# One of the six low parts of each expert chunk is made by GpSimd instead of VectorE

## The reference, cut to what matters

```
def swiglu(h, wg, wu, wd):
    a = jnp.einsum('bsd,df->bsf', h, wg)
    b = jnp.einsum('bsd,df->bsf', h, wu)
    return jnp.einsum('bsf,fd->bsd', jax.nn.silu(a) * b, wd)

def moe_swiglu(h, router_w, wg, wu, wd):
    ...
    for e in range(N_EXPERTS):
        out = out + combine[..., e:e + 1].astype(h.dtype) * swiglu(h, wg[e], wu[e], wd[e])
```

## Time and profile before

| | us |
|---|---|
| median of 3 runs | 1541.75 (1541.41 to 1542.61) |
| the profiled execution: its own time | 1544.39 |
| its span, first to last instruction | 1542.6 |
| expert stage, roughly | from 540 to 1528 |
| one plain step of six tiles | 17.0 |
| one scatter step | 18.9 |

### The profile page before, as it was taken

The page is one execution under the profiler, slowest core; times in us unless marked ns, Lnnn a source line. Parts: engine busy times, 40 slices in busy tenths (PEclk is TensorE's granted clock), DMA queues, the critical chain, the costliest instruction groups (busy, mean ns, idle before and its releaser), DMA issues.

```text
span 1542.6 us, 19268 instructions
## 1 busy us (share of the span) xinstructions
PE 1503.1 (97%) x7347; PEld 1243.0 (81%) x7347; DVE 1190.7 (77%) x881; ACT 975.6 (63%) x742; POOL 11.0 (1%) x26
## 2 busy tenths in 40 slices
PE   7999999999999999999999999999999999999996
PEld 5987788888888678888878888887888888888885
DVE  4777454444787588898888889888889888888885
ACT  4565433344556477777767776776777777777774
POOL 2000000000000000000000000000000000000000
PEclk9999999999999999999999999999999999999998
DMA  9624555554552279999999999999999998999991
GB/s 312 217 96 139 177 191 189 189 190 137 178 177 96 96 271 387 372 361 360 376 324 336 373 375 351 369 335 327 373 366 350 372 376 316 359 365 377 355 375 61
DMA packets 190583, 437.70 MB, mean 284 GB/s; under 512 B 9328, under 2 KB 13472, under 8 KB 190384
## 3 DMA queue, kind: packets, MB, share of 16 engines
q1 hardware_dynamic: 189024, 432.90, 78.0%
q0 software_dynamic: 1056, 2.19, 0.7%
q10 hardware_dynamic: 432, 1.57, 0.3%
HBM read 435.59 MB, written 1.05 MB: 283 GB/s over the span
## 4 chain that ended last, share of the span: by engine, by line
PE 91%; DVE 4%; issue 2%; ACT 2%; DMA 1%; SPq 0%; DVEq 0%; ACTq 0%
PE ps L1219 28%; PE ps L1221 28%; PE ps L1220 28%; PE ps L1523 2%; DVE w_lo L1068 1%; DVE w_lo L760 1%; PE ps L1480 1%; PE ps L1498 1%; DMA raw<-in_w_in_dram 1%; PE ps L1499 1%; ACT w_hi L584 0%; PE ps L1282 0%; PE ps L1281 0%; PE ps L1280 0%; ACT w_hi L440 0%
## 5 line engine op out<-in xcount | busy, mean ns | idle before, releaser
L1068 DVE TENSOR_TENSOR w_lo<-raw,w_hi 128x2048 fp32r<-128x2048 f32 x333 | 754.1, 2288 | 111.9 <-ACT w_hi L584 110.9
L584 ACT ACTIVATE w_hi<-raw 128x2048 fp32r<-128x2048 f32 x332 | 630.4, 1920 | 171.7 <-PE ps L1221 171.7
L1219 PE MATMUL ps<-w_hi,aT_hi 128*128 128x512 f32 (+1 forms) x1296 | 512.8, 396 | 13.9 <-DVE w_lo L760 6.1
L1221 PE MATMUL ps<-w_hi,aT_lo 128*128 128x512 f32 (+1 forms) x1296 | 504.6, 389 | 0.0
L1220 PE MATMUL ps<-w_lo,aT_hi 128*128 128x512 f32 (+1 forms) x1296 | 503.1, 388 | 0.0
L1219 PEld LDWEIGHTS ps<-w_hi,aT_hi 128*128 128x128 f32 x1296 | 244.0, 188 | 68.3 <-issue 11.6
L1221 PEld LDWEIGHTS ps<-w_hi,aT_lo 128*128 128x128 f32 x1296 | 243.8, 188 | 53.0
L1220 PEld LDWEIGHTS ps<-w_lo,aT_hi 128*128 128x128 f32 x1296 | 244.2, 188 | 48.7
L760 DVE TENSOR_TENSOR w_lo<-raw,w_hi 128x2048 fp32r<-128x2048 f32 (+2 forms) x81 | 176.9, 2186 | 109.5 <-ACT w_hi L440 109.3
L440 ACT ACTIVATE w_hi<-raw 128x2048 fp32r<-128x2048 f32 (+2 forms) x81 | 148.0, 1830 | 117.1 <-PE ps L1221 110.8
L1219 PE MATMUL ps<-w_hi,s2T_hi 128*128 128x512 f32 x544 | 213.8, 393 | 1.5 <-DVE s2T_lo L773 1.5
(11 more groups left out here) (260 smaller groups left out, 897.3 us busy)
## 6 DMA issues: line engine op xcount, KB each, us to landing
raw<-in_moe_w_gate_dram SPq DMA_DIRECT2D x112, 1024.0 KB, 6.9
raw<-in_moe_w_up_dram SPq DMA_DIRECT2D x112, 1024.0 KB, 7.5
raw<-in_moe_w_down_dram SPq DMA_DIRECT2D x112, 1024.0 KB, 7.0
raw<-in_w_in_dram SPq DMA_DIRECT2D x20, 1024.0 KB, 6.0
raw<-in_ffn_w_gate_dram SPq DMA_DIRECT2D x14, 1024.0 KB, 5.0
raw<-in_ffn_w_up_dram SPq DMA_DIRECT2D x14, 1024.0 KB, 5.0
raw<-in_ffn_w_down_dram SPq DMA_DIRECT2D x14, 1024.0 KB, 4.7
raw<-in_w_out_dram SPq DMA_DIRECT2D x8, 1024.0 KB, 5.0
```

The source lines that it names most:

```text
L584: nc.scalar.activation(moe_hi(pos), raw[:, slot, :], ACT.Copy).then_inc(hi_ready, 1)
L1068: V.tensor_tensor(moe_lo(pos), raw[:, pos % 6, :], moe_hi(pos).bitcast(F32), ALU.subtract)\
L1219: mm(out, lhs_hi, rhs_hi, start=start, stop=False, skip_group_check=True)
L1221: return mm(out, lhs_lo, rhs_hi, start=False, stop=stop, skip_group_check=True)
```

## The change

The low part of tile 3 of each step, the second down tile, is taken out of VectorE's order, in both bodies of `pair`, and given to GpSimd, as the same subtraction on the same buffers with the same semaphores before and after it. GpSimd reads the number of pairs as the other engines do and runs through a loop of its own: 14 subtractions in each of the first three pairs, and 13 in the last. The very last chunk's second down tile is split at another place of the code and stays on VectorE. So 55 of the 56 are moved. Nothing else is changed: no buffer, no order on TensorE, ScalarE or the transfer queue.

```
+            def down_low_parts(p, count):
+
+                g0 = MOE_BASE + p * (6 * PAIR)
+                for k in range(1, count):
+                    pos = 6 * k + 3
+                    pool.wait_ge(hi_ready, g0 + (pos + 1))
+                    nc.gpsimd.tensor_tensor(moe_lo(pos), raw[:, pos % 6, :], moe_hi(pos).bitcast(F32), ALU.subtract)\
+                        .then_inc(lo_ready[pos % 6], 1)
+
+            pool.wait_ge(routed, 1)
+            last = pool.value_load(n_items[0:1, 1:2], min_val=E // 2 - 1, max_val=E - 1)
+            with pool.Fori(0, last) as p:
+                down_low_parts(p, PAIR + 1)
+            down_low_parts(last, PAIR)
...
                     evac_sT(k)
                     add_block0(k)
-                    lo(6 * k + 3)
                     lo(6 * k + 4)
...
                     evac_sT(k)
-                    lo(6 * k + 3)
                     lo(6 * k + 4)
                     gate_times_up(k)
```

## The result

Before, the kernel took 1542.18 us (median of 4 runs), with the change 1553.9 us (4 runs, 1550.77 to 1556.67). The ratio is 1.0056, 95% interval 1.0039 to 1.0074: slower, as forecast, inside the range, and by somewhat more than the forecast 0.4%. The two medians alone would give 1.0076; with four runs on each side, spread over 4.0 and 5.9 us, 0.4 to 0.8% is what can be said. In the repetition further down, three single executions (one each of the kernel before, a_after and e5_after_cast_first) took 3048 to 4153 us, and all medians and ratios leave them out. The profiled execution took 1550.77 us with a span of 1548.9 us.

What follows compares the result with a forecast made beforehand. The prediction took TensorE as the bound, with VectorE's work hidden behind it. Profiled 1544.39 + 0 (plain) + 0 (scatter) + 6.4 (gathers) = 1550.8, less 2.64 for the median: 1548.2 us; range 1540 to 1568.

Steps and rivals of the forecast that it cites:

- VectorE's work is hidden, so taking it away gains nothing: Expert stage: the 121 us of low parts leaving VectorE lie under TensorE's work and are worth nothing by themselves.
- The operation takes 4.35 us and fits into 5.15: Plain step: GpSimd's subtraction ends before TensorE's first matmul on tile 3, 0.8 us to spare, costing 0 us.
- Turns: Low parts 3 and 4: VectorE waits until GpSimd's read of the same memory is done, starting 2.15 us later.
- GpSimd is then always first: Order of turns in each step: GpSimd leads, since high part 3 comes 1.8 us before high part 4.
- The shift fits in the other places: Plain and scatter steps and reloads: low parts 2.15 us later still end before TensorE wants them, 0 us.
- Three gathers x 2.15 us: At the gathers VectorE's late low part 4 delays TensorE by as much: 6.4 us in all.
- The sum, 1548.2 us: Whole kernel: 1544.39 + 0 + 0 + 6.4 = 1550.8 us profiled, less 2.64 for the median, 0.4% slower.
- Rival C: Plain steps: the operation is not ready in 5.15 us, TensorE waits in 44 steps, 1569 to over 1600; chance 0.31.
- B: No interference: VectorE runs on beside GpSimd, waits at the gathers shrink by 1.4 us, 1540.4 us; chance 0.22.

Runs made afterwards that it cites:

- a_after: The changed kernel again, unaltered, in the repetition on another chip: 1555.8 us, ratio 1.0077 to the kernel before.
- e5_after_cast_first: The changed kernel with VectorE's first cast of gathered tokens moved ahead of low part 5 in step 13: 1543.55 us, ratio 1.0001 to the kernel before.
- e1: The changed kernel with step 13 of the first three pairs back on VectorE, 52 low parts on GpSimd: 1545.03 us, ratio 1.0005 to the kernel before.
- e8: The changed kernel with step 13's low part on VectorE and the first cast ahead of low part 5: 1541.36 us, ratio 0.9978 to the kernel before.
- e6: The changed kernel with an extra GpSimd subtraction of 512 columns right before each of its 55 low parts: 1621.93 us, ratio 1.0517.
- e2: The kernel before with only step 13 of the first three pairs on GpSimd, 3 operations of 55: 1554.84 us, ratio 1.0069.
- e10: The kernel before plus a one-column GpSimd subtraction and a 2047-column copy on constants in 42 steps: 1546.5 us (before 1546.03).

## Why the prediction was right, point by point

- **VectorE's work is hidden, so taking it away gains nothing.** Right: e1 and e8 show it, with 52 low parts moved and a stage as long as without the move.
- **The operation takes 4.35 us and fits into 5.15.** Right, and its size 0.3 us low: 4.64 at the median, starting 0.08 us behind high part 3. It ends about 0.4 us before the budget does in 41 of the 44 steps. e6 shows that the budget is real: 5.95 us make TensorE wait in 44 steps, the number counted.
- **Turns.** The choice between turns and no interference was a choice, and it was right: 5.03 us for low part 4 in place of 2.29. Only where to see it was left open, and it is the duration that grows. "GpSimd is then always first" was wrong in three steps of 55.
- **The shift fits in the other places.** Right but for one place, which the prediction did not look at: in the step where VectorE also builds the selection matrices, it is still at low part 2 when high part 3 is ready, and GpSimd comes second. In the scatter step the result's low part is begun at 925.81 and ends at 927.02, some 0.5 us before TensorE's scatter, as worked out, and no wait appeared.
- **Three gathers x 2.15 us.** Right in place, low in size: 2.34 us each, 7.0 us instead of 6.4, from the longer operation. e2 puts the whole loss on these three.
- **The sum, 1548.2 us.** 5.7 us below the median. 0.6 us of that is the operation's size. A term was missing: the granted clock at a long wait, 1.7 us for each stretch of 3.4 us at half clock, which the profiles show at one gather in the changed kernel and, 5.1 us in all, at two in e2. It shows at none in the kernel before or where the wait is filled or under 1 us. The stage of the profile adds up with it: 7.0 us at the gathers, 1.7 of clock and 0.5 in the three steps, less 1.0 of the waits "issue", make 8.2 of the 8.3 us by which it grew. That the profiled span grew by 6.3 us, nearly the sum, is partly luck: the part ahead of the stage was 2.0 us shorter. The base was low as well: the forecast starts from a median of three runs, 1541.75 us, and the kernel before had medians of 1544.3 to 1546.0 us on the three chips of the experiments. What else the median holds I can't tell from four runs whose clocks are 0.988 to 0.992.
- **Rival C** did not happen in 41 of the 44 plain steps, with 0.4 us to spare. In the other three its condition "VectorE gets the turn first" came true, at a cost of less than 0.2 us each. B did not happen.

## What to carry to other kernels

Moving an operation with two inputs in SBUF from VectorE to GpSimd does not free VectorE when more of the same kind follow: while GpSimd reads, VectorE's own two-input operations are blocked, so here a 4.6 us operation on GpSimd takes more of VectorE's time (2.7 us of blocking) than the 2.3 us that it took there. Before such a move look for the places where VectorE's chain is the last to end, in the waits of the bounding engine, however short they are: a wait of 0.7 us, three times in 1000 us, was the only sign among TensorE's waits, and the same sign pointed at the reordering that made the kernel 0.2% faster. Look also where VectorE has extra work: there it runs late, and the order of the turns can change. A blocked instruction looks busy; compare its duration with its minimum.

## What was not expected of the hardware

- A subtraction of a single column on GpSimd took 2.30 us because it came 0.04 us behind VectorE's; the shortest took 0.19.
- At TensorE's waits of 3.05 us the granted clock fell to half, 1.2 GHz, at three of the six gathers in two profiles: for some 3.4 us behind two of the waits, and for some 6.8 us at the third, where it fell 0.6 us before the wait ended. It fell behind one of three waits of 1.82 us too (e10). In the profiles it did not fall at waits of 0.7 to 0.9 us, nor when matmuls on zeros filled the wait.
- VectorE's blocked low part ends 2.15 us behind GpSimd's end, a little less than the 2.28 it takes alone.
- Two GpSimd subtractions waited for two low parts of VectorE in a row, 9.03 us each instead of 4.64, though their records begin 0.05 us ahead of VectorE's.
